# Hymba-style decoder step: each sample's main cache copy on GpSimd's DMA queue as one transfer of 2.2 or 2.3 MB

## The reference, cut to what matters

```python
def trunk_layer(x, start_pos, conv_buf, pool_buf, k_buf, v_buf, ...):
    ...
    kk = jnp.concatenate([k_buf, k], axis=1)
    vv = jnp.concatenate([v_buf, v], axis=1)
    o = dilated_attention(q, kk, vv, k_buf.shape[1])
    ...
    new_k = kk[:, -n_keep:]          # n_keep = 2048
    new_v = vv[:, -n_keep:]
    y = jnp.einsum('bte,ed->btd', jnp.concatenate([ya, yb, yc], axis=-1), w_out)
    return x + y, new_conv, new_pool, new_k, new_v
```

## Time and profile before

| what | value |
|---|---|
| time, median of 3 runs | 404.59 us (402.63 to 405.35) |
| time of the profiled execution | 401.57 us |
| its span, first to last instruction | 399.7 us |
| TensorE busy | 347.5 us (87%) |
| VectorE busy | 232.6 us (58%) |
| GpSimd busy | 58.8 us (15%), 110 instructions |
| moved by the 16 DMA engines | 157.73 MB, mean 395 GB/s |
| of it by GpSimd's queue (q0) | 14,624 packets, 88.25 MB |

### The profile page before, as it was taken

How to read it: one execution, slowest core, us unless ns; L and a number is a source line. 1 busy time by engine, 2 the same in 40 slices (tenths; PEclk the granted TensorE clock), 3 DMA queues, 4 the chain that set the end, 5 groups by cost and what they waited for, 6 DMA issues and landing times.

```text
span 399.7 us, 4745 instructions
## 1 busy us (share of the span) xinstructions
PE 347.5 (87%) x1550; PEld 273.4 (68%) x1550; DVE 232.6 (58%) x530; ACT 100.2 (25%) x237; POOL 58.8 (15%) x110
## 2 busy tenths in 40 slices
PE   3898799999889859899948999999979877989990
PEld 2686578887667636588827888888757654758870
DVE  2604669859977976620103489978984997541010
ACT  4200012542523123500111011453352222320011
POOL 4006830000600002044000420000600011000000
PEclk9999969999889899999986999999979988989997
DMA  8999999999999999999999999999999999999983
GB/s 293 412 419 412 418 418 417 418 407 411 417 419 408 418 392 406 396 418 418 416 398 387 414 418 416 417 411 420 418 419 417 414 357 361 372 374 372 396 347 118
DMA packets 44329, 157.73 MB, mean 395 GB/s; under 512 B 6988, under 2 KB 20116, under 8 KB 44306
## 3 DMA queue, kind: packets, MB, share of 16 engines
q0 software_dynamic: 14624, 88.25, 54.6%
q10 hardware_dynamic: 14420, 41.52, 26.3%
q1 hardware_dynamic: 15262, 27.67, 18.7%
HBM read 140.23 MB, written 104.46 MB: 612 GB/s over the span
## 4 chain that ended last, share of the span: by engine, by line
PE 43%; DVE 13%; SPq 12%; ACTq 11%; DMA 10%; issue 5%; ACT 4%; DVEq 0%
PE pj L693 23%; SPq L479 11%; DMA kg<-in_cache_k_win 10%; PE pj L836 8%; ACTq L459 4%; DVE yc L1296 3%; ACTq L465 3%; PE psc L765 3%; PE ptr L611 3%; DVE ssc L1240 2%; ACTq L463 2%; PE ps L813 1%; ACTq L874 1%; DVE spsum_pad L1266 1%; DVE tok L1234 1%
## 5 line engine op out<-in xcount | busy, mean ns | idle before, releaser
L693 PE MATMUL pj<-hT,wt 128*128 128x264 f32 x800 | 197.9, 407 | 6.3 <-DVE hT L1151 4.5
L693 PEld LDWEIGHTS pj<-hT,wt 128*128 128x128 f32 x800 | 159.0, 202 | 39.7 <-issue 11.6
L1296 DVE SCALAR_TENSOR_TENSOR yc<-u_ext,par,yc 128x256 f32<-128x256 f32 x180 | 77.2, 481 | 3.8 <-DVE u_smp L1180 1.0
L836 PE MATMUL pj<-mix,wt 128*128 128x264 f32 x256 | 61.2, 395 | 0.0
L836 PEld LDWEIGHTS pj<-mix,wt 128*128 128x128 f32 x256 | 49.1, 194 | 8.5
L600 POOL DMA_DIRECT2D out<-in_cache_v_win x48 | 26.2, 554 | 142.3 <-issue 142.3
L1366 DVE TENSOR_TENSOR xT<-xT,pj 128x264 f32<-128x264 f32 x16 | 6.9, 430 | 55.9 <-PE pj L836 55.9
L600 POOL DMA_DIRECT2D out<-in_cache_k_win x48 | 26.5, 561 | 83.6 <-issue 83.6
L954 ACT ACTIVATE ex<-pj 128x264 f32<-128x264 f32 x22 | 8.6, 391 | 78.3 <-PE pj L693 45.2
L1178 DVE SCALAR_TENSOR_TENSOR u_ext<-ex,pj 128x256 f32<-128x256 f32 x6 | 2.5, 422 | 30.5 <-ACT ex L954 30.5
L1234 DVE TENSOR_TENSOR tok<-kg,qb 128x1536 f32<-128x1536 f32 x10 | 17.6, 1758 | 3.4 <-DMA kg<-in_cache_k_win 3.0
(11 more groups left out here) (187 smaller groups left out, 339.6 us busy)
## 6 DMA issues: line engine op xcount, KB each, us to landing
wt<-in_w_tiles ACTq DMA_DIRECT2D x62, 512.0 KB, 33.2
out<-in_cache_k_win POOLq DMA_DIRECT2D x24, 1080.0 KB, 44.4
out<-in_cache_v_win POOLq DMA_DIRECT2D x24, 1080.0 KB, 81.1
out<-in_cache_k_win POOLq DMA_DIRECT2D x8, 1200.0 KB, 72.7
out<-in_cache_v_win POOLq DMA_DIRECT2D x8, 1200.0 KB, 87.9
out<-in_cache_k_win POOLq DMA_DIRECT2D x16, 432.0 KB, 65.1
out<-in_cache_v_win POOLq DMA_DIRECT2D x16, 432.0 KB, 86.2
kg<-in_cache_k_win SPq DMA_DIRECT2D x32, 144.0 KB, 36.0
```

What stands on the lines that cost most here:

```text
L693: last = nc.tensor.matmul(pj[n % RING][:, 0:T], wt[:, g % WRING, k, :], hT[:, k, :], start=(k == 0), stop=(k == KD - 1))
L836: last = nc.tensor.matmul(pj[n % RING][:, 0:T], wt[:, g % WRING, k, :], mix[:, k, :], start=(k == 0), stop=(k == KD - 1))
L1296: last = V.scalar_tensor_tensor(out=yc[:, t, 0:SEQ], in0=x_w, scalar=par[:, ROW_CW + w * CT + t:ROW_CW + w * CT + t + 1], in1=yc[:, t, 0:S ...
```

## The change

Each sample's main part becomes one transfer in place of two: rows 0 to 1536 of a layer-1 cache (2160 KB) or rows 0 to 1520 of a layer-0 cache (2280 KB). The length of the runs, the rows that are copied and their order by sample stay. There are 64 transfers in place of 96, so `STATE_STORE` is renumbered: both stores of the states stand between the same rows as before (after the main part of the third k cache of layer 1, and after the second k cache of layer 0).

```diff
@@ -207,14 +207,12 @@
 
 DEEP = (("k", 1), ("v", 1))
 EVEN_ROWS = (FAR_LO - 1) // (16 * PIECE_ROWS) * 16 * PIECE_ROWS
-EVEN_CUT = EVEN_ROWS // (32 * PIECE_ROWS) * 16 * PIECE_ROWS
 
 
 def copies_of(l):
 
     return [(kind, s, a, b) for kind in ("k", "v") for s in range(NS)
-            for a, b in (*(((0, FAR_LO // 2), (FAR_LO // 2, FAR_LO)) if (kind, l) in DEEP else ((0, EVEN_CUT), (EVEN_CUT, EVEN_ROWS))),
-                         (FAR_LO, GATHER[0][0]))]
+            for a, b in ((0, FAR_LO if (kind, l) in DEEP else EVEN_ROWS), (FAR_LO, GATHER[0][0]))]
 
 
 COPIES = {l: copies_of(l) for l in range(DEPTH)}
@@ -242,7 +240,7 @@
 
 SHARES = {"conv_w": ((0, 80), (80, CONV_W * CT))}
 
-STATE_STORE = {8: 0, 54: 1}
+STATE_STORE = {5: 0, 36: 1}
 STATE_CUTS = ((1, 113), (113, 120))
```

## The result

| | before | changed |
|---|---|---|
| median of 20 runs each | 405.13 us | 406.75 us |
| ratio, 95% interval | | 1.0051 (1.0031 to 1.0071) |
| profiled execution, its span | 401.57, 399.7 us | 407.95, 406.1 us |

The change makes the kernel about 2 us (half a per cent) slower. That is within the 1% that I called no change, and inside the range; but the forecast leaned to 0.3 us faster, and 20 runs are enough to show that it went the other way. Of the kernels with the copies alone (group 2), three runs that lie over 1.5% above the fastest of their kernel are in the slow state and left out of medians and ratios.

The account below looks back on a forecast made before the run. The DMA engines were taken as the first bound, with compute and lagging engines ending together. All terms were 0 except 0.3 us gained at transfer ends: 401.57 to 401.3 profiled, 404.3 us forecast as median, range 400.5 to 408.

Parts of the forecast that it names:

- how the DMA engines are shared: In busy stretches engines take one packet of each queue in turn, whatever the transfer's size; q0 keeps 55.8%; worth 0.
- the ring: POOL's descriptor ring: room for some 256 packets an engine; when full, POOL waits for the copy 16 back; q0 never dry.
- compute ends at 391 in any case: At the kernel's end: stores of y must land after compute, so no more than about 4 us can be gained.
- The sign: Whole kernel: the terms sum to 0.3 us faster, with the profiled execution going from 401.57 to 401.3 us.
- Two things thus end together: At the kernel's end: compute ends at 391 us, and the DMA engines that are behind end some us later.
- The ends of transfers: On q0: each transfer's end costs 0 to 0.1 us, 0 to 3.2 us over 32 transfers; 0.3 us gain taken.
- The landings: Copies issued from 48.60 us: pieces took 4.7 and 2.4 us against 4.6 and 2.35 by turns, leaving 0 to 0.1 us.
- POOL's instructions: On POOL: 32 fewer DMA instructions save 17.8 us of its time, all hidden because it idles before copies; worth 0.
- the states: Stores of the states on POOL: wait reached near 122 us, lasting until the same 171.7; worth 0.
- Rival 1: At 320 to 380 us: wider address spacing disturbs HBM, 7 us more, 411 us; slower by over 1%, chance 0.10.
- Rival 2: At 320 to 380 us: copies run better, at most about 4 us gained, 400.5 us; upper half, chance 0.12.
- Rival 3: On the DMA engines: longer turns per queue raise q0's share to 72%, about 20 us more, 425 us; chance 0.02.

Follow-up runs that it names:

- group 2: Four kernels with everything but GpSimd's cache copies left out, in the forms before, changed, two transfers with changed chunks, and three transfers; medians 279.42, 280.28, 279.88 and 280.40 us.
- e1: The changed kernel measured again without edits, against the kernel before: ratio 1.0057 (1.0029 to 1.0086).
- e2: Against the kernel before: two transfers per main part still, but each engine's chunk of the cache as in the changed kernel; ratio 1.0031 (1.0011 to 1.0051).
- a3: The changed kernel measured again without edits on another chip, against the kernel before: ratio 1.0025 (0.9997 to 1.0054).
- e9: Two transfers per main part with each engine's chunk as in the changed kernel, measured once more against the kernel before: ratio 1.0024 (0.9998 to 1.0050).
- b1_before_again: The kernel before, measured again without edits on the chip of its group: ratio 0.9996 (0.9971 to 1.0022).
- a2_after_again: The changed kernel measured again without edits, against the kernel before on the same chip: ratio 1.0025 (1.0003 to 1.0047).
- e6_six: Six transfers per main part, 224 copies in all, against the kernel before with 96: ratio 1.0139 (1.0107 to 1.0172).
- e4: Three transfers per main part, 128 copies in all, against the kernel before: ratio 1.0012 (0.9991 to 1.0032).

## Why the prediction was wrong

- **The step that failed** is the one on how the DMA engines are shared. It found the right rule, one packet of each queue in turn, and then concluded that "the size of a transfer is not in this rule", and took 0. It is in the rule, since the end of a transfer is itself a packet on each engine, the one that counts up the semaphore, and it takes one of q0's turns while moving 4 bytes. I had counted those packets in two places (for the ring, and as the 512 that would be missing), but not as turns. The share of engine time, which I kept at "55.8%", was 56.2% before and 57.0% after over 50 to 200 us. With it fell the premise "compute ends at 391 in any case": on one chip the last matmul went from 390.9 to 397.0 us.
- **What it is worth** can be estimated from rows that were there. In the earlier trace rows, q10 and q1 use 33.3% and 13.7% of 16 engines for 10 us with 385 and 384 packets: 0.138 + 0.057 = 0.195 us of an engine for one turn of both. 32 ends fewer an engine are 32 turns that SP's and ACT's queues do not get while q0 moves the same rows: 32 x 0.195 = 6.2 us. Measured: the last matmul 6.1 us later than in the kernel before on one chip, and 5.8 us (e1 against e2) and 4.6 us (a3 against e9) later than in the form with 96 transfers and the same chunks on two others.
- **Why only about 2 of the 6 us show.** My reading of the end was right: two things end together, compute with its stores, and what the DMA engines have left. Before, the stores of `vg` and the copies were the later ones; the last store of y went out at 394.3 us in b1_before_again and 8 us passed to the end. In a2_after_again it goes out at 399.6 and only 3 us pass:

```profile
394.27 0.36 SPq L557 DMA_DIRECT2D out<-qk  x1
...
399.56 0.35 SPq L555 DMA_DIRECT2D out<-qk  x1
```

So the change takes 3 us off the copies' end, adds 6 to compute's, and the kernel ends by the one that got worse. The spans of these two executions are 402.2 and 402.7 us; the medians are 1.5 us apart (404.13 and 405.59).
- **The sign.** I saw that "Two things thus end together" and then only asked what the change does to the copies. At such a tie a shift of bandwidth to one side soon makes the other the end, so there is little to gain either way: one transfer gave 1.0025 to 1.0057 and six 1.0139, and three, at 1.0012 (0.9991 to 1.0032), cannot be told from none.
- **The ends of transfers** as a fixed cost (0.3 us taken, 3.2 at most): the copies alone with 128 and with 64 transfers differ by 0.1 us, and a packet of 4 bytes is recorded with 9 ns, so the low end was right for q0 by itself. The landings held the missing turn, but the working hid it. It took 4096 and 1536 bytes for every turn of q10 and q1, where the earlier trace rows has 1.36 MB / 385 = 3530 and 0.51 MB / 384 = 1330 on average. With 0.195 us for a turn of both, and q0's own time from the same rows (0.232 us for 6050 bytes), nine rounds of the 1080 KB piece take 4.4 us and six of the far one 2.2. The landings were 4.7 and 2.4: by this estimate 0.3 and 0.15 us are left, on average one more turn of the others, and not the 0.1 us at most that I had found.
- **POOL's instructions, the ring, the states** (0 each): right as far as the time shows. POOL was busy for 43.0 us in 78 instructions (forecast 41 to 45), came to the wait for the states at 120.7 us (122) and sent its last DMA at 306.4 (305); only the states' load landed later than forecast, at 177.1 and not 171.7 us.
- **Rival 1** (order of addresses, slower) had the right sign for a reason that was not shown: the copies alone are as fast in both forms as far as can be told, and at 320 to 380 us the rate after is the 371 GB/s of the row below against 373 in the earlier trace rows. Earlier the two pages differ more (405 against 417 GB/s at 230 to 320 us), but that is mostly the two executions: on one chip it is 409 before and 406 after at 200 to 320 us. The cost of 0.2 to 0.3% in e2 and e9 is left open, and with it a part of the changed kernel's. **Rival 2**: the laggards' backlog shrank, but compute then was the end. **Rival 3**: refuted by the equal counts, as the trace before said. Yet it was the same mechanism, turns of the queues, and I had priced it only for the case that the turns became longer, not for the case that q0 wastes fewer of them.

The stretch of the changed kernel that answers to the third of the earlier trace rows:

```profile
320.00:380.00 60.00, 50.89 (x247) 37.00 (x247) 36.78 (x82) 13.85 (x30) 0.00 (x0) 0.94 1.02 371
```

## What to carry to other kernels

Where several queues are backlogged on the same DMA engines and take turns packet by packet, count the packets that each queue needs for its bytes, with those that end a transfer: in this kernel that count set its share. Fewer, longer transfers then raise the share of their queue at the expense of the others, so merge, if any, those of the queue that the end waits for. Cutting the background copies finer has its own limit: three transfers in place of two gained nothing that can be told, and six lost 1.4%. And where two streams end together, ask of a change what it does to each of them; a gain for one that is paid by the other is a loss.

## What was not expected

- A turn that moves 4 bytes is worth 0.195 us of the other queues' time on an engine, so 32 transfers fewer move the last matmul by 4.6 to 6.1 us, 32 more by 5.6 us the other way (387.1 in e2 to 381.5 in e4), while the copies by themselves do not notice 64 of them (280.28 and 280.40 us).
- POOL's stops can be counted ahead: by estimate room for about 256 packets an engine, and at a full ring a wait for the copy whose semaphore was used longest ago, 16 copies back. Ten of the eleven stops of over 1 us in the changed kernel end 0.3 to 0.4 us after that copy's landing. The last is one: the copy issued at 200.07 us landed 104.4 us later, at 304.5, and POOL went on at 304.82.
- The copies alone run at 317 GB/s, under the 410 and more of the mix, with all engines busy (98.1%). So time at the end in which only copies are left may be dear. e6_six is 5.9 us slower than b1_before_again although its compute is done 9 us earlier; how much of that comes from this rate is not shown, as its engines still wrote 380 and 373 GB/s at 384 to 392 us, and after that fewer and fewer of them had work (share 0.83 at 392 to 396 us, 0.34 at 396 to 400).
